# Two PSUM banks for SSD's y, its scores beside the transposes of B, other tiles for early output copies, and row exponentials between GLA's copies

## What is computed

```python
# SSD, per chunk l of a sequence
acum = cumsum(dt * A)
cb = einsum('lgn,sgn->lsg', C, B)                         # scores
decay = where(causal, exp(acum[l] - acum[s]), 0)
y_intra = einsum('lsh,sh,shp->lhp', cb * decay, dt, x)
states = einsum('lh,lhn,lhp->hpn', exp(acum[-1] - acum) * dt, B, x)
h = h * exp(acum[-1]) + states                            # from chunk to chunk
y_inter = einsum('lhn,hpn,lh->lhp', C, h_prev, exp(acum))
y = y_intra + y_inter + D * x                             # then * silu(z), a norm, w_out
# GLA
o = o_intra + o_inter                                     # then a norm, * silu(gate), w_out
out = concat([y_ssd, o_gla, o_fox]) @ w_out
```

## Time and profile before

| | us |
|---|---|
| median of 3 runs (lowest to highest) | 2020.12 (2017.82 to 2020.54) |
| the profiled execution | 2020.3 |
| its span | 2018.5 |
| TensorE's matmuls busy | 1980.7 |
| VectorE busy | 1183.8 |
| ScalarE busy | 777.0 |
| GpSimd busy | 235.5 |

### The profile page before, as it was taken

One profiled execution on the slowest core, in us unless ns is written; L12 is line 12 of the kernel. 1 busy time (PEld: TensorE's weight loads), 2 busy tenths in 40 slices (PEclk: granted clock), 3 DMA queues, 4 the chain that ended last, 5 costly groups with the idle time before them and its releaser, 6 DMA issues.

```text
span 2018.5 us, 36227 instructions
## 1 busy us (share of the span) xinstructions
PE 1980.7 (98%) x15386; PEld 1930.6 (96%) x15386; DVE 1183.8 (59%) x1613; ACT 777.0 (38%) x1248; POOL 235.5 (12%) x285
## 2 busy tenths in 40 slices
PE   7999999999999999999999999999999999999999
PEld 7899999999999989868899989999999999999999
DVE  5955655556766752564455283377555565577674
ACT  6433333334433342563333483243333333343331
POOL 0000000000000340250012172100000000000000
PEclk9999999999999999999999999999999999999999
DMA  4222232224976514211011253312322223388664
GB/s 153 82 87 102 87 114 98 87 102 174 381 270 234 212 43 192 80 53 43 24 45 43 68 147 131 128 51 105 111 87 85 99 103 113 117 318 325 249 218 161
DMA packets 74352, 268.48 MB, mean 133 GB/s; under 512 B 8724, under 2 KB 27588, under 8 KB 64848
## 3 DMA queue, kind: packets, MB, share of 16 engines
q1 hardware_dynamic: 58928, 202.30, 27.8%
q0 software_dynamic: 15264, 63.87, 8.2%
HBM read 206.92 MB, written 59.22 MB: 132 GB/s over the span
## 4 chain that ended last, share of the span: by engine, by line
PE 92%; DVE 4%; ACT 2%; issue 1%; DMA 1%; POOL 0%; SPq 0%; DVEq 0%; ACTq 0%
PE ps L169 85%; PE ps L1538 1%; PE ps L1494 1%; PE ps L1520 1%; PE ps L247 1%; DVE sb_x L509 0%; PE ps L2146 0%; DVE sb_xl L563 0%; PE ps L2152 0%; DVE sb_xl L499 0%; PE ps L2162 0%; DMA sb_x<-x 0%; DVE sb_x L548 0%; PE ps L2133 0%; PE ps L2169 0%
## 5 line engine op out<-in xcount | busy, mean ns | idle before, releaser
L169 PE MATMUL ps<-sb_xh,sb_up_hi 128*128 128x272 f32 x2400 | 691.2, 288 | 6.4 <-DVE sb_x L2539 2.0
L169 PE MATMUL ps<-sb_xl,sb_up_hi 128*128 128x272 f32 x2400 | 691.5, 288 | 0.0
L169 PE MATMUL ps<-sb_xh,sb_up_lo 128*128 128x272 f32 x2400 | 689.5, 287 | 0.0
L169 PEld LDWEIGHTS ps<-sb_xh,sb_up_hi 128*128 128x128 f32 x2400 | 452.3, 188 | 7.8 <-DVE sb_up_lo L454 2.3
L169 PEld LDWEIGHTS ps<-sb_xh,sb_up_lo 128*128 128x128 f32 x2400 | 451.8, 188 | 0.0
L169 PEld LDWEIGHTS ps<-sb_xl,sb_up_hi 128*128 128x128 f32 x2400 | 451.5, 188 | 0.1
L169 PE MATMUL ps<-sb_h_hi,sb_down_hi 128*128 128x272 f32 x1188 | 342.5, 288 | 0.4 <-DVE sb_down_lo L1049 0.4
L169 PE MATMUL ps<-sb_h_hi,sb_down_lo 128*128 128x272 f32 x1188 | 342.8, 289 | 0.0
L169 PE MATMUL ps<-sb_h_lo,sb_down_hi 128*128 128x272 f32 x1188 | 341.7, 288 | 0.0
L169 PE MATMUL ps<-sb_nh,sb_whi 128*128 128x362 f32 (+1 forms) x696 | 232.6, 334 | 1.9 <-DVE sb_nl L376 1.5
L169 PE MATMUL ps<-sb_nl,sb_whi 128*128 128x362 f32 (+1 forms) x696 | 229.6, 330 | 0.0
(11 more groups left out here) (347 smaller groups left out, 2692.4 us busy)
## 6 DMA issues: line engine op xcount, KB each, us to landing
sb_down_raw<-wb SPq DMA_DIRECT2D x92, 704.0 KB, 5.3
sb_up_raw<-wa SPq DMA_DIRECT2D x44, 1024.0 KB, 4.8
sb_h_raw<-h_kept SPq DMA_DIRECT2D x60, 544.0 KB, 6.2
sb_wraw<-wm SPq DMA_DIRECT2D x17, 1024.0 KB, 4.7
h_kept<-sb_hs_b POOLq DMA_DIRECT2D x20, 816.0 KB, 4.8
h_kept<-sb_hbuf POOLq DMA_DIRECT2D x42, 272.0 KB, 2.3
h_kept<-sb_hs_a POOLq DMA_DIRECT2D x20, 544.0 KB, 3.2
sb_h_first_raw<-h_kept SPq DMA_DIRECT2D x10, 544.0 KB, 4.6
```

The source lines that it names most:

```text
L169: mm = K.nc.tensor.matmul(out, a, b, start=first and n == 0, stop=last and n == 2, skip_group_check=loose)
```

## The change

The exponentials of `K.ge` and `K.ga` move from behind GLA's ninth copy to behind the copies of tiles 2 and 4. y of tile j lies in bank 5 or 4 by the parity of j, and the D term waits for the z product of two tiles before. The scores of tile j (except tile 0, which stays in bank 4) lie in the bank of the transposes of B of the same tile, columns 256 to 511; they wait for that tile's copy of B in place of `M.m`. The early output copies and their subtractions run at tiles 2, 3, 5 and 7 in place of 2, 3, 4 and 5.

```diff
 def gla_act(K, e, M):
     nc.scalar.preload_act_table_set(LOG_EXP)
+    g = slice(SMALL_DT, SMALL_DT + SSD_H)
     for j, (a, r) in enumerate(TILES):
         e.wait_ge(M.go_mm, j + 1)
         nc.scalar.copy(K.go[:, :, a:a + r], K.ps[:, 4:6, :r]).then_inc(M.go_read, 1)
-    g = slice(SMALL_DT, SMALL_DT + SSD_H)
-    e.wait_ge(M.acum, 1)
-    nc.scalar.activation(K.ge[g, :], K.adt[g, :], ACT.Exp).then_inc(M.gexp, 1)
-    nc.scalar.activation(K.ga[g, :], K.to_end[g, :], ACT.Exp).then_inc(M.gexp, 1)
+        if j == 2:
+            e.wait_ge(M.acum, 1)
+            nc.scalar.activation(K.ge[g, :], K.adt[g, :], ACT.Exp).then_inc(M.gexp, 1)
+        if j == 4:
+            nc.scalar.activation(K.ga[g, :], K.to_end[g, :], ACT.Exp).then_inc(M.gexp, 1)
...
+def ssd_scores_at(K, j):
+    bank, at = (4, 0) if j == 0 else (tile_banks(j)[1], 256)
+    return K.ps[:, bank, at:at + 2 * P].rearrange("p (u q) -> p u q", u=2)
+
+def ssd_y(K, j):
+    return K.ps[:, 5 - j % 2].rearrange("p (t q) -> p t q", t=4)
+
+def mix_early_at(j):
+    return EARLY_TILES.index(j) if j in EARLY_TILES else None
...
 def ssd_cb_pe(K, e, M, j):
     a, r = TILES[j]
-    wait(e, M.m, j)
+    if j:
+        e.wait_ge(M.b_read, j + 2)
     for u in range(2):
-        mm = K.nc.tensor.matmul(K.ps[:r, 4, P * u:P * u + r], K.xc[:, 4 + u, a:a + r],
+        mm = K.nc.tensor.matmul(ssd_scores_at(K, j)[:r, u, :r], K.xc[:, 4 + u, a:a + r],
...
     def back(j):
-        wait(e, M.y2, j)
-        y = K.ps[:, 5].rearrange("p (t q) -> p t q", t=4)
+        wait(e, M.y2, j - 1)
+        y = ssd_y(K, j)
...
-        if j >= 2 and j - 2 < len(MIX_EARLY):
-            k = MIX_EARLY[j - 2]
+        if mix_early_at(j) is not None:
+            k = MIX_EARLY[mix_early_at(j)]
...
+EARLY_TILES = (2, 3, 5, 7)
```

More of the change, by code:

```diff
@@ L2349, in state @@
         V.tensor_tensor(K.z[:, :, a:a + r], K.z[:, :, a:a + r],
-                        K.ps[:, 5].rearrange("p (t q) -> p t q", t=4)[:, :, :r], ALU.mult).then_inc(M.y2, 1)
+                        ssd_y(K, j)[:, :, :r], ALU.mult).then_inc(M.y2, 1)
     def tokens(j):
@@ L2373, in decayed @@
         e.wait_ge(M.cb2_mm, j + 1)
-        cbm = K.ps[:r, 4, :2 * P].rearrange("p (u q) -> p u q", u=2)
+        cbm = ssd_scores_at(K, j)[:r]
         M.dve(V.tensor_tensor(cbm[:, :, :r], cbm[:, :, :r],
@@ L2432, in ssd_pool @@
             norm(y_after(j, 3))
-        if j >= 2 and j - 2 < len(MIX_EARLY):
-            k = MIX_EARLY[j - 2]
-            e.wait_ge(M.mhi_early, j - 1)
+        if mix_early_at(j) is not None:
+            k = MIX_EARLY[mix_early_at(j)]
+            e.wait_ge(M.mhi_early, mix_early_at(j) + 1)
             G.tensor_tensor(K.nl[:, k], mixed_tile(K, k), K.nh[:, k].bitcast(F32), ALU.subtract)\
```

## The result

The changed kernel takes 2025.28 us (median of 21 runs) against 2018.86 us for the kernel before (21 runs of the same set): a difference of 6.4 us in the medians. The ratio on record, which leaves out the one run in a slow state (2143.32 us), is 1.0028, 95% interval 1.0022 to 1.0034, or some 5.6 us. The kernel is slower, by more than the 0.2% that can be told from no change, and outside the range of 2018.2 to 2023.4. A second set (8 runs against 24) gave 2024.27 against 2019.5 us, ratio 1.0020 [1.0009, 1.0030]. The profiled execution took 2026.43 us (span 2024.7), 6.1 more than the one of before.

A forecast was written before the change was run, and what follows sets the result against it. TensorE, busy 98% of the span, was taken as the bound, with 2.2 us of visible idle in SSD. Terms -1.0 + 1.7 + 0 + 0.1 = +0.8 us took the median from 2020.12 to 2020.9; range 2018.2 to 2023.4.

The forecast's parts named there:

- GLA's exponentials: End of GLA: TensorE's stall before the sums at L1898 goes, -1.0 us; GpSimd's two later instructions 0, bounds 0 and +0.3.
- The scores' wait: Head of SSD: tile 1's scores wait for ScalarE's copy of B, +1.7 us, bounds +1.5 and +1.9; later tiles cost nothing.
- Rival C: Head of SSD: the stall doesn't come, as tile 1's copy is earlier than read; 2019.1 us, chance 0.04.
- y in two banks: SSD's D term: the wait only moves behind it, since xde ends last; 0 us, bounds 0 and -1.6.
- rival A: SSD: two banks do free TensorE, z's waits of 1.6 to 3.1 us go; 2017.8 to 2019.3 us, chance 0.11.
- Early output tiles: SSD tiles 6 to 8: moved subtractions shift GpSimd's holds on VectorE's product L2340; +0.1 us, bounds -1.0 and +2.4.
- rival B: SSD tiles 6 and 8: GpSimd holds VectorE's state product, 4.9 us together; 2025.7 at the end, 2023.3 with half; chance 0.15.
- The chances: Whole kernel: slower by over 4 us 0.05, faster by over 4 us 0.03, within 0.92.

The follow-up runs named there:

- experiment 5: Changed kernel with y in one bank again, the D term waiting for z of the tile before; 2023.79 us, ratio 1.0025.
- Experiment 7: Changed kernel with tile 1's copy of B first, early tiles back at 2 to 5, and z behind the next tile's tokens; 2016.58 us, ratio 0.9988.
- Both filled: Changed kernel with unread products filling TensorE's waits before tile 1's scores and the last tile's states; 2021.41 us, ratio 1.0004.
- 8: Kernel before with only the early output tiles moved to 2, 3, 5 and 7; 2024.19 us, ratio 1.0018.
- 9: Kernel before with early output tiles moved and four unread products filling TensorE's wait before the last tile; 2020.52 us, ratio 1.0006.
- 1: Kernel before with one line added: scores of tile 1 also wait for ScalarE's copy of B; 2022.40 us, ratio 1.0015.
- 6: Changed kernel with ScalarE's copy of B of tile 1 first and early tiles back at 2 to 5; 2018.15 us, ratio 0.9994.
- 4: Changed kernel with four unread products filling TensorE's wait before tile 1's scores; 2023.41 us, ratio 1.0017.
- 10: Changed kernel with only ScalarE's copy of B of tile 1 put first, early tiles left at 2, 3, 5, 7; 2023.51 us, ratio 1.0016.
- 3: Kernel before with only the two row exponentials moved behind GLA's copies of tiles 2 and 4; 2018.95 us, ratio 0.9998.
- 2: Changed kernel with the early output tiles back at 2, 3, 4 and 5; 2023.10 us, ratio 1.0016.

## Why the prediction was wrong

**GLA's exponentials: right.** -1.0 forecast, -0.95 measured in the stretch (22.16 to 21.21), the copies still every 1.68 us; nothing of the bound of +0.3 for GpSimd's two later instructions shows.

**The scores' wait: right as a wait.** +1.7 forecast with bounds 1.5 and 1.9; the head of the profiles with full clock is 7.66 - 5.89 = 1.77 us longer, and the delay stays to the end of SSD. From tile 2 on no scores wait, as forecast. Rival C (2019.1 us; 2019.2 by its own sum) falls: the copy ran where it was read to run.

**y in two banks: right, and for the reason given.** 0 forecast. The wait moved from before the D term to before the states (L2171 waits in tiles 2, 3, 5, 7 and 8, each for xde), experiment 5 undoes it without a loss, so rival A falls. One number of the working is off, on the safe side: without its wait of 0.64 us the D term of tile 5 would have ended at 1185.11, not 1185.75. Experiment 7 bears out the sentence behind it, that VectorE's chain is the longer: with z out of the way and a state product of 0.69 us, the loop comes to 2.85 us, TensorE's own way as it was read from the earlier trace rows.

**Early output tiles: the step was mis-sized.** I took +0.1, with an upper bound of +2.4. Measured, with both waits filled and so with the clock out of it: from the states of tile 1 to those of tile 8 are 56.55 - 7.66 - 3.90 = 44.99 us, and 53.14 - 5.89 - 3.90 = 43.35 before, so +1.64 (by the same differences +0.4 to +2.1 in the seven profiles of the table in which the copy was held for 2.7 us, and -0.5 to +0.6 in the four others with the early tiles where they were and z in its old place). I looked for the hold at the state product L2340 alone, in tiles 6 and 8, and let small overlaps of both signs cancel. What was held is the plain copy behind that product, L2347, which only tile 8 has and which my text didn't name. No state product of the changed kernel's SSD took over 1.6 us. (The 0.69 us that I read between the end of the subtraction and that of the product beside it is 0.56 by the earlier trace rows, 1189.98 less 1189.42; 0.69 is the length of a product that nothing holds, as in the first row of experiment 7.) It was rival B's mechanism at an instruction that B hadn't listed, and one such place, priced at up to 2.5 us, is what came. The copy ends at 1206.73, 0.29 us after the subtraction (1206.44); alone it takes 0.92. The Trainium skill (SBUF — State Buffer, section "SBUF: two separate sides") says that GpSimd and VectorE's operations in a two-port mode hold a port pair by turns, for a whole instruction. The trace agrees, with the 0.92 and 2.68 us above; I had used the rule for an operation with two operands and not asked which others it covers.

**The step that failed: every wait was priced at its own length.** -0.95 + 1.77 + 0 + 1.64 is +2.5 us, or 2022.6 by the prediction's own reckoning: inside the range. "Both filled" runs at 1.3 us above before, with an interval of -1.0 to +2.4 whose upper end this sum just about meets. The changed kernel, at 4.8 to 6.4 above before, is 3.5 to 5.1 us slower than "both filled". No term of the sum, no bound and no rival had the granted clock in it, although was read for it: the clock was 1.00 over the stretch, and I took this for a constant. Here it fell behind waits. In the first profile the low clock costs 1.38 us at the head (9.04 against 7.66) and 1.57 at the tail (5.47 against 3.90).

The record also has the mean granted clock of every execution, to three decimals. On average it is 0.9968 over the changed kernel's runs behind the ratio (0.9971 in its second set) and 0.9989 with both waits filled; the kernels before of the sets that have it are at 0.9986 to 0.9989. What is missing to 1, times the time, is what a TensorE that is always busy would lose: 6.5 us (5.8), against 2.2 with both filled. That is an estimate of 3.7 to 4.3 us for the clock, beside the 3.5 to 5.1 in the medians. In 8 and 9 the means are 0.9969 and 0.9982, or 2.6 us by the same working. The head's wait alone (1) has 0.9985 against 0.9988, only some 0.6 us, which with its 2.08 us of delay makes its 2.7. These means don't say where in an execution the clock was low.

**The chances** failed with it: a twentieth for slower rested on B's holds alone, 3.3 us of them; one hold with its clock is 4.5 us (experiment 8).

What is shown and what isn't: that the low clock hangs on the wait is shown at the tail, by filling it (experiments 8 and 9, one edit apart, 3.5 us). At the head it is shown less well, since there the clock falls in some executions only and the mean clock of 1 is hardly lower. That each loss is worked off by mending its place is shown for both together (6). How the two combine in the changed kernel, less than their sum, stays open.

## What to carry to other kernels

On a kernel whose TensorE is busy for 98% at full clock, price a new wait of 2 us not only at 2 us, but also at the case that the clock halves behind it: here 1.4 to 3.2 us more where it fell. When an operation on GpSimd is moved, write down every VectorE instruction that will lie beside it, plain copies included, and not only the one that was seen to be held. A second buffer can pay once the order on the engine that ends last is changed to use it: the second bank of y was worth nothing until z stood behind the tokens, and after that the stretch between head and tail was 1.7 us shorter, as the medians were by 1.6 (2018.15 to 2016.58, with overlapping intervals).

## What the hardware showed that was not expected

The granted clock fell to its lower level in the stretch after a wait of TensorE, in some executions and not in others. Before the last tile: after waits of 2.1 to 2.6 us in all five profiles that have one unfilled (both of the changed kernel, 4, 8, 10), after waits of 0.9 to 1.0 us in two of three (3 and 6, not 5), after 0.72 or less in none of six (before, 1, 2, 7, 9, 12). At the head, after waits of 1.75 to 1.84 us, in two of five (the first profile of the changed kernel and 5; not 1, 2 or its second profile). In 7 a wait of 1.2 us, before the last sums, was followed by no low clock. One wait that no edit touches shows the same thing: at the start of the second SwiGLU block TensorE waits 1.99 us for VectorE (L2539 before, L2559 after) in all fourteen profiles, at full clock until then. In ten of them the granted clock over the 8 us behind it was 0.79, and 51 matmuls ran in them; in the other four (before, 3, 5 and 7) it was 1.00, with 62 matmuls. So a single profile can differ from another by this much with nothing changed there. The low stretch need not begin at the wait's end: in the first profile of the changed kernel TensorE resumed at 1208.62 at full clock, and the sums of 1210.87 ran at half. The Trainium skill (TensorE: Matmul & The Clock Gate, section "What's actually happening") has a gate before the array that passes half or all of the clock by how busy the engine was; the two levels are those of the rows here, 0.50 and 1.00.
